# Row broadcast of the reciprocal roots: one plain four-byte product in place of two rounded ones

## The reference

```
def rms_norm(x, g):
    xf = x.astype(jnp.float32)
    y = xf * lax.rsqrt(jnp.mean(xf * xf, axis=-1, keepdims=True) + RMS_EPS)
    return (y * g.astype(jnp.float32)).astype(x.dtype)

def swiglu(x, w_in, w_out):
    gu = x @ w_in
    g, u = jnp.split(gu, 2, axis=-1)
    return (jax.nn.silu(g) * u) @ w_out
...
for l in range(DEPTH):
    x = x + 0.5 * swiglu(rms_norm(x, ffn1_norm[l]), ffn1_w_in[l], ffn1_w_out[l])
    x = x + mixer(rms_norm(x, mix_norm[l]), ...)
    x = x + 0.5 * swiglu(rms_norm(x, ffn2_norm[l]), ffn2_w_in[l], ffn2_w_out[l])
```

## Time and profile before

| | |
|---|---|
| median of three runs | 2212.1 us |
| the profiled execution | 2212.68 us, of which span 2210.9 us |
| granted TensorE clock | 1.0 |
| busy: PE / PEld / DVE / ACT | 99% / 94% / 78% / 51% of the span |
| chain that ended last | PE 92%, DVE 5%, ACT 1%, issue 1% |

### The profile page before, as it was taken

How to read it: one execution, slowest core, us unless ns; L and a number is a source line. 1 busy time by engine, 2 the same in 40 slices (tenths; PEclk the granted TensorE clock), 3 DMA queues, 4 the chain that set the end, 5 groups by cost and what they waited for, 6 DMA issues and landing times.

```text
span 2210.9 us, 44748 instructions
## 1 busy us (share of the span) xinstructions
PE 2198.9 (99%) x17380; PEld 2088.0 (94%) x17380; DVE 1721.4 (78%) x2840; ACT 1132.8 (51%) x1503; POOL 2.6 (0%) x9
## 2 busy tenths in 40 slices
PE   9999999999999999999999999999999999999999
PEld 8999999999999999999999889999999998999998
DVE  7778668778777758777877988887787788888876
ACT  5445465445445565444444676654454446766443
POOL 0000000000000000000000000000000000000000
PEclk9999999999999999999999999999999999999999
DMA  7555445554555445654556444455555545445653
GB/s 256 192 199 196 171 160 198 199 196 166 208 199 193 171 154 186 221 190 170 192 189 220 173 146 142 171 201 189 184 183 207 185 175 179 146 144 173 217 199 133
DMA packets 76818, 407.64 MB, mean 184 GB/s; under 512 B 9265, under 2 KB 9921, under 8 KB 44337
## 3 DMA queue, kind: packets, MB, share of 16 engines
q1 hardware_dynamic: 75792, 404.93, 51.9%
q10 hardware_dynamic: 720, 0.89, 0.1%
q0 software_dynamic: 208, 0.49, 0.1%
HBM read 405.23 MB, written 1.05 MB: 184 GB/s over the span
## 4 chain that ended last, share of the span: by engine, by line
PE 92%; DVE 5%; issue 1%; ACT 1%; DMA 0%; DVEq 0%; SPq 0%; ACTq 0%
PE ps_aux L694 13%; PE ps_proj L685 13%; PE ps_y L263 10%; PE ps_y L264 10%; PE ps_y L265 10%; PE ps_aux L697 7%; PE ps_proj L689 7%; PE ps_proj L1131 3%; PE ps_proj L1138 3%; PE ps_proj L1132 3%; PE ps_proj L263 1%; PE ps_proj L265 1%; PE ps_proj L264 1%; DVE w_lo_front L130 1%; PE ps_aux L651 1%
## 5 line engine op out<-in xcount | busy, mean ns | idle before, releaser
L105 ACT CAST w_hi_front<-w_raw_front 128x2048 fp32r<-128x2048 f32 x238 | 453.4, 1905 | 285.3 <-PE ps_aux L697 252.9
L130 DVE TENSOR_TENSOR w_lo_front<-w_raw_front,w_hi_front 128x2048 fp32r<-128x2048 f32 x238 | 544.0, 2286 | 56.8 <-ACT w_hi_front L105 56.7
L263 PE MATMUL ps_y<-hidden_lo,w_hi_back 128*128 128x256 f32 x1344 | 372.4, 277 | 0.1
L264 PE MATMUL ps_y<-hidden_hi,w_lo_back 128*128 128x256 f32 x1344 | 371.1, 276 | 0.0
L265 PE MATMUL ps_y<-hidden_hi,w_hi_back 128*128 128x256 f32 x1344 | 371.1, 276 | 0.0
L105 ACT CAST w_hi_back<-w_raw_back 128x1024 fp32r<-128x1024 f32 x248 | 260.2, 1049 | 153.5 <-PE ps_y L265 126.3
L694 PE MATMUL ps_aux<-xt_lo_hi,w_hi_front 128*128 128x512 f32 x1280 | 319.5, 392 | 0.0
L685 PE MATMUL ps_proj<-xt_lo_hi,w_hi_front 128*128 128x256 f32 x2560 | 316.6, 276 | 0.0
L130 DVE TENSOR_TENSOR w_lo_back<-w_raw_back,w_hi_back 128x1024 fp32r<-128x1024 f32 x248 | 301.6, 1216 | 2.3 <-ACT w_hi_back L105 1.8
L685 PEld LDWEIGHTS ps_proj<-xt_lo_hi,w_hi_front 128*128 128x128 f32 x2560 | 302.4, 188 | 0.0
L888 ACT ACTIVATE silu_gate<-silu_gate 128x256 f32<-128x256 f32 x176 | 73.7, 419 | 383.5 <-DVE silu_gate L931 351.5
(11 more groups left out here) (491 smaller groups left out, 3746.1 us busy)
## 6 DMA issues: line engine op xcount, KB each, us to landing
w_raw_front<-in_stream SPq DMA_DIRECT2D x251, 1024.0 KB, 4.9
w_raw_back<-in_stream SPq DMA_DIRECT2D x252, 512.0 KB, 4.3
m_rel_bias<-in_rel_bias SPq DMA_DIRECT2D x2, 2048.0 KB, 9.7
m_params<-in_params SPq DMA_DIRECT2D x2, 656.0 KB, 5.0
w_raw_front<-in_stream SPq DMA_DIRECT2D x4, 256.0 KB, 7.1
w_raw_front<-in_stream SPq DMA_DIRECT2D x2, 512.0 KB, 8.8
x<-in_x ACTq DMA_DIRECT2D x3, 256.0 KB, 7.0
out<-x SPq DMA_DIRECT2D x3, 256.0 KB, 2.3
```

The lines of the kernel that those rows point to most:

```text
L105: self.nc.scalar.copy(self.hi[part][:, parity], self.raw[part][:, parity]).then_inc(self.hi_done[part], by)
L130: eng.tensor_tensor(self.lo[part][:, parity], self.raw[part][:, parity], self.hi[part][:, parity].bitcast(F32), ALU.subtract).then_inc(sel ...
L263: nc.tensor.matmul(out, ah, bl, start=start, stop=False)
L264: nc.tensor.matmul(out, al, bh, start=False, stop=False)
```

## The change

The high and low parts of the reciprocal and the rounded identity are gone, with three semaphores. `column_rows` makes one product for each column, of the plain 4-byte `inv_rms` and the plain identity. A tile without a use (`gap_norms`) of the same size as the three removed ones keeps every other tile in its place.

```diff
@@ shared_state @@
-    s.rcol_hi = sb("inv_rms_hi", [P, 2 * TT], F32R)
-    s.rcol_lo = sb("inv_rms_lo", [P, 2 * TT], F32R)
-    s.ident_r = sb("identity_rounded", [P, P], F32R)
+    sb("gap_norms", [P, 4 * TT + P], F32)
...
@@ inverse @@
     s.nc.vector.reciprocal(s.rcol[:, 0:width], s.rms[:, 0:width]).then_inc(s.rcol_ready, 1)
-    s.nc.vector.wait_ge(s.rcol_ready, n + 1)
-    s.nc.vector.tensor_copy(s.rcol_hi[:, 0:width], s.rcol[:, 0:width]).then_inc(s.rcol_rounded, 1)
-    s.nc.vector.wait_ge(s.rcol_rounded, n + 1)
-    s.nc.vector.tensor_tensor(s.rcol_lo[:, 0:width], s.rcol[:, 0:width],
-                              s.rcol_hi[:, 0:width].bitcast(F32),
-                              ALU.subtract).then_inc(s.rcol_split, 1)
@@ column_rows @@
-        s.nc.tensor.matmul(toks, s.rcol_lo[:, col].to_broadcast([P, P]), s.ident_r[:],
-                           start=True, stop=False)
-        last = s.nc.tensor.matmul(toks, s.rcol_hi[:, col].to_broadcast([P, P]), s.ident_r[:],
-                                  start=False, stop=True)
+        last = s.nc.tensor.matmul(toks, s.rcol[:, col].to_broadcast([P, P]), s.ident[:])
@@ spread_rows, spread_first @@
-    s.nc.tensor.wait_ge(s.rcol_split, n + 1)
+    s.nc.tensor.wait_ge(s.rcol_ready, n + 1)
@@ ffn_start @@
-    pe.wait_ge(s.ident_rounded, 1)
+    pe.wait_ge(s.ident_came, 16)
@@ ffn_vector, n = 0 @@
-        dve.wait_ge(s.ident_came, 16)
-        nc.vector.tensor_copy(s.ident_r[:], s.ident[:]).then_inc(s.ident_rounded, 1)
```

More of the change, by code:

```diff
@@ L306, in shared_state @@
     s.rcol_ready = sem("rcol_ready")
-    s.rcol_rounded = sem("rcol_rounded")
-    s.rcol_split = sem("rcol_split")
     s.rows_done = sem("rows_done")
@@ L2725, in build @@
         s.ident_came = sem("ident_came")
-        s.ident_rounded = sem("ident_rounded")
         s.half_hi = sem("half_hi")
```

## The result

The changed kernel takes 2262.72 us (median of 4 runs, 2262.53 to 2263.38) against 2212.19 us of the kernel before (4 runs, 2212.08 to 2213.11): ratio 1.0229, 95% interval 1.0216 to 1.0241. It is 2.3% slower, 50.5 us. The forecast was 2211.8, and the range ended at 2214.7.

What follows compares the result with a forecast made beforehand. TensorE was taken to bound the kernel (busy 2198.9 of 2210.9 us). Products 0, X2 wait -0.30 and start +0.05 gave -0.25 us, so 2211.8 off the 2212.1 median, range 2209.5 to 2214.7.

Steps and rivals of the forecast that it cites:

- the fourth: Rival, all 13 spreads: plain records with a repeated column as stationary operand go at 0.216, +5.5 us, 2217.3; chance 0.04.
- The products, taken at 0: TensorE's 13 spreads: 52 rounded records become 52 plain ones at about the same pace; 0 us, near bounds -0.3 to +0.5.
- rivals 3 and 4: Spreads' plain 128-wide records dearer: 3, full 0.108 streaming, +2.8 us, chance 0.06; 4, pace 0.216, +5.5 us, chance 0.04.
- the fifth: Rival: in the spreads, a plain product could be more than two records; given no chance of its own.
- The rule of four passes: Four-byte floats pass TensorE's array four times; by it alone the spreads' sum would be 2.8 us higher.
- The wait at X2, -0.30: Norm X2: TensorE no longer waits for the low part, only for the reciprocal, already there; -0.30 us.
- VectorE's 4.9 us, hidden: Twelve norms' two short instructions and the identity's rounding go from VectorE; nearly all lies beside other work, gain 0.
- the start, +0.05: At the start the spread's rows come later, and the chain to TensorE's wait at L854 is not hidden: +0.05 us.
- rival 2: VectorE's removed time counts in full: -4.9 us, so 2207.2, faster by 0.22%; chance 0.04.
- The sum, -0.25: Whole kernel: products 0, X2 wait -0.30, later rows at the start +0.05; -0.25 us, called no change.
- the marks named for the forecast: Changed profile: 52 records 0.11 apart, no reciprocal wait at X2, 0.9 to 1.0 idle before mixers' L568, start wait 0.05 longer.
- the mark against it: Forecast wrong if spread records are 0.15 or more apart, or a new TensorE wait over 1 us appears.

Runs made afterwards that it cites:

- e2: Kernel before with all its instructions, two small tiles made into one so later tiles, moving operands included, stand 32 bytes lower: 2262.70 us, 1.0225 of before.
- e1: Changed kernel with its gap tile 32 bytes longer, so all tiles stand where the kernel before has them: 2212.61 us against 2212.85.
- e10: Changed kernel with tiles restored, but `hidden_hi`, `hidden_lo`, the identity and a few small tiles 32 bytes higher: 2250.07 us against 2213.01.
- e8: Changed kernel with a larger gap tile, moving operands 128 bytes above their place in the kernel before: 2238.56 us against 2213.50.
- e3: Changed kernel with rounded weights and moving operands both 32 bytes lower than in the kernel before, their distance unchanged: 2212.18 us against 2212.85.
- e9: Changed kernel with a larger gap tile, moving operands 256 bytes above their place in the kernel before: 2211.90 us against 2213.01.

## Why the prediction was wrong

**The step that failed.** It stands in no line of the sum, because it was taken for granted: that outside the spreads TensorE's products cost what they cost before. It was said as "nothing else has moved", for the order of the instructions, and as the gap tile that keeps the other tiles in place, for memory. The first is true and the second was added up in bytes of the tiles (16 + 16 + 512 = 544), not in what the tiles take as built (32 + 32 + 512 = 576), so that the operands of TensorE came to stand 32 bytes nearer to each other. The missing term is 17380 records at some 3 ns, 50.5 us, and e2 shows it whole without any of the change's instructions. No rival held it either; the fourth had the right sign, but the wrong place: a plain record at 0.216.

**The terms of the sum.** They can be read in e1, which has the changed instructions in the old layout.

*The products, taken at 0: right.* Timeline of e1, mixer 2, TensorE and then VectorE:

```profile
1234.79 0.60 PE L596 MATMUL ps_y<-identity,inv_rms 128*128 128x128 f32 x4
1235.15 0.36 PE L263 MATMUL ps_aux<-xt_lo_hi,w_hi_back 128*128 128x256 f32 x1
1235.36 0.28 PE L264 MATMUL ps_aux<-xt_lo_hi,w_lo_back 128*128 128x256 f32 x1
...
1235.44 0.42 DVE L558 COPY inv_rms_rows<-ps_y 128x256 f32<-128x256 f32 x1 [1.02 <-PE ps_y L596]
```

There are 52 records of L596 in all, the four of a spread 0.11 apart, and 0.57 us from the first to the second product of weights, as in the earlier trace rows. So rivals 3 and 4, dearer plain records, did not occur, nor did the fifth. The rule of four passes (the Trainium skill, page "FP8 and Floating Point Precision", section "TensorE Precision Notes") makes nothing dearer here: a spread of two plain products lasts as long as one of four rounded ones (0.57 us). And the copy of the rows now stands 1.02 idle where it stood 0.54: VectorE's saved 0.4 us became waiting, as forecast.

*The wait at X2, -0.30: right.* Timeline of e1 at X2:

```profile
1051.89 0.39 PE L638 MATMUL ps_aux<-xt_lo_hi,w_hi_front 128*128 128x512 f32 x1
1052.12 0.60 PE L596 MATMUL ps_y<-identity,inv_rms 128*128 128x128 f32 x4
1052.48 0.47 PE L638 MATMUL ps_aux<-xt_lo_hi,w_hi_front 128*128 128x512 f32 x1
```

The spread starts 0.23 behind the product ahead of it, with no idle time in brackets, where its weight load waited 0.34 in the earlier trace rows. TensorE's lead over the kernel before grows there by 0.33 (from 0.37 to 0.70). It does not last to the end: both spans are 2210.9 us.

*VectorE's 4.9 us, hidden; the start, +0.05: right.* Timeline of e1, the start and the feed-forward part n = 2:

```profile
20.70 0.42 DVE L912 TENSOR_TENSOR silu_gate<-silu_gate,ps_y 128x256 f32<-128x256 f32 x1 [0.75 <-PE ps_y L596]
...
352.20 0.28 PE L644 MATMUL ps_proj<-xt_lo_hi,w_lo_front 128*128 128x256 f32 x1
...
352.52 0.69 DVE L906 TENSOR_REDUCE silu_gate<-ps_proj 128x256 f32<-128x512 f32 x1 [0.47 <-PE ps_proj L644]
```

L906 starts 0.04 behind the end of L644 (352.20 + 0.28), exactly as its forerunner did in the earlier trace rows, and now with 0.47 idle ahead of it that ends with TensorE. At the start L912 waits 0.75 instead of 0.29 for the rows, and TensorE's lead shrinks by 0.05. VectorE is busy 4.2 us less (1717.2 against 1721.4; the forecast's 4.9 counted the gaps between the removed instructions too) and the whole is not faster by that: rival 2 did not occur.

*The sum, -0.25.* e1 against before is -0.24 between the medians, with an interval of 0.999 to 1.0008 (2 us each way), and the two profiled executions last 2212.69 and 2212.68 us. That the medians meet the forecast is luck: a stretch behind a spread that goes slow in one kernel and fast in the other, as at n = 3 and n = 5 above, moves TensorE's lead by 0.2 us, nearly the whole sum.

So each step that was worked out held at its own place, and the result was missed by 51 us through one that was not looked at. In the changed profile the marks named for the forecast appeared, near enough (the copy of the rows in mixer 2 has 1.07 idle before it where 0.9 to 1.0 was named); the mark against it, a spread of slower records or a wait over 1 us, did not. The even growth of the delay, over products that were not touched, is what should make a reader leave the change and look at what they share.

**What stays open.** That the 32 bytes between the weights and the moving operands make the 50 us is shown, and that 256 bytes more give the time of before while the six other shifts do not. Why is not. In e1 the weight load of L264 runs from 1235.24 to 1235.43, beside the product L263 from 1235.15 to 1235.51, so that two reads of the same memory that fall on each other would be a guess; no run here separated the reads of TensorE from each other, or from what other engines do to the tiles that moved along. Nor is it shown why the slow pace outlasts its cause (e10), what starts and ends it in the fast layout, or why e8's down projection is slow at a rest at which the gate is fast. No layout that was run is faster than that of the kernel before: e1, e3 and e9 equal it.

## What to carry to other kernels

Before a removed or added tile is called neutral, list the address of every tile in both built programs and compare them; a sum of tile sizes is not that list. When a kernel that TensorE bounds moves by per cents and the delay grows evenly over untouched products, compare the starts of the same products first, and run the old instructions in the new layout and the new ones in the old: two runs separate a change from its side effect. When tiles are added, keep the distance between weights and moving operands, or change it by 256 bytes, which in this kernel gave the time of before (e9), or try a few values of it on purpose.

## What the hardware showed that was not expected

- Back-to-back rounded products 256 wide go at 113.5 ns or at 117 to 120 ns at the same granted clock of 1.0. The distance of the two operands in a partition, shifted for all products at once, takes the kernel from 2212 to 2282 us (3.2%) at the worst of the eight shifts that ran (0 among them).
- Slow products slow others whose operands have not moved: 37 us in e10 where the moved pairs account for 19. In the kernel before, one and the same list of 16 products takes 1.88 us behind one spread and 1.82 behind another.
- A plain four-byte product 128 wide is two records 0.11 apart, and two such products take the time of four rounded ones (0.57 us up to the second product behind them). Halving the number of products in a spread gave nothing and cost nothing that can be told.
